# Another order for matmul groups that fill waits: token mixing and modulation units around layer 0's attention

## The reference

```python
# layer 0 mixer, per token tile; h = modulated rms_norm(x)
z = h @ w_in
u, v, q, k, vv = split(z)                 # 512, 512, 512, 128, 128 columns
v = layer_norm(gelu(v), g_vnorm)
mixed = einsum('gts,bnsgc->bntgc', w_s, v_chunks) + b_s
a_out = gelu(u) * mixed
q, k = rms_norm(q, g_q), rms_norm(k, g_k) # latents: then apply_rope on both
b_out = attention with sinks (prompt: dense; latents: window + 128 context keys)
y = concat([a_out, b_out]) @ w_o
# both layers
sh1, sc1, g1, sh2, sc2, g2 = split(silu(cond) @ w_ada + b_ada)
x = x + g1 * y
x = x + g2 * hier_moe(rms_norm(x, g_norm2) * (1 + sc2) + sh2)
```

## Time and profile before

| | |
|---|---|
| three runs | 1081.3, 1087.42, 1085.52 us, median 1085.52 |
| profiled execution | 1081.3 us, of which span 1079.5 |
| mean granted TensorE clock | 0.926 |
| TensorE busy | 913.2 us, 85% |
| VectorE, ScalarE, GpSimd busy | 387.9, 238.7, 120.6 us |
| DMA | 324.97 MB, mean 301 GB/s |

### The profile page before, as it was taken

How to read it: one execution, slowest core, us unless ns; L and a number is a source line. 1 busy time by engine, 2 the same in 40 slices (tenths; PEclk the granted TensorE clock), 3 DMA queues, 4 the chain that set the end, 5 groups by cost and what they waited for, 6 DMA issues and landing times.

```text
span 1079.5 us, 14089 instructions
## 1 busy us (share of the span) xinstructions
PE 913.2 (85%) x5389; PEld 522.4 (48%) x5389; DVE 387.9 (36%) x1096; ACT 238.7 (22%) x598; POOL 120.6 (11%) x131
## 2 busy tenths in 40 slices
PE   5999798977999985998399979997869998859980
PEld 2346346446555553554165544553565555525540
DVE  1112565246522120221334665661456222212214
ACT  3110143120111110111334454341111111101111
POOL 1000001000222211121000000001001222112210
PEclk9999899987999997998699997998869999989996
DMA  9979897385989998998740057008499899999984
GB/s 379 399 294 403 318 417 308 103 276 211 373 313 401 415 416 361 416 413 343 297 149 6 1 193 275 10 7 286 181 404 366 330 410 417 416 392 409 413 338 182
DMA packets 69835, 324.97 MB, mean 301 GB/s; under 512 B 12566, under 2 KB 13590, under 8 KB 46600
## 3 DMA queue, kind: packets, MB, share of 16 engines
q1 hardware_dynamic: 54016, 291.99, 68.0%
q0 software_dynamic: 13328, 25.02, 6.8%
q10 hardware_dynamic: 2432, 7.17, 1.7%
HBM read 318.97 MB, written 26.49 MB: 320 GB/s over the span
## 4 chain that ended last, share of the span: by engine, by line
PE 64%; DMA 21%; DVE 9%; ACT 2%; issue 2%; SPq 1%; POOL 0%; POOLq 0%; DVEq 0%; ACTq 0%
PE psum L760 16%; DMA ring<-in_l_w 13%; PE psum L773 8%; PE psum L956 7%; PE psum L710 4%; DMA ring<-in_l_w_ada 3%; PE psum L1048 3%; PE psum L740 2%; PE psum L1057 2%; PE psum L1008 2%; PE psum L601 2%; PE psum L1089 2%; PE psum L723 1%; DMA scale_shift<-gate_rows_hbm 1%; PE psum L731 1%
## 5 line engine op out<-in xcount | busy, mean ns | idle before, releaser
L760 PE MATMUL psum<-ring,scratch 128*64 128x256 f32 x1920 | 226.8, 390 | 24.6 <-DMA ring<-in_l_w 22.8
L760 PEld LDWEIGHTS psum<-ring,scratch 128*64 128x64 f32 x1920 | 143.6, 140 | 92.9 <-issue 35.2
L1902 DVE TENSOR_TENSOR scratch<-scratch,psum 64x256 f32<-64x256 f32 x64 | 27.2, 424 | 315.0 <-ACT scratch L1304 314.9
L773 PE MATMUL psum<-ring,scratch 128*64 128x512 f32 x496 | 119.9, 604 | 2.6 <-ACT scratch L1308 1.9
L2336 POOL DMA_INDIRECT expert_rows<-scratch,slot_rows x64 | 63.7, 995 | 333.2 <-ACT scratch L1318 321.5
L1304 ACT ACTIVATE scratch<-psum 64x256 f32<-64x256 f32 x64 | 24.0, 375 | 258.4 <-PE psum L760 258.4
L956 PE MATMUL psum<-ring,scratch 128*128 128x512 f32 x192 | 73.1, 539 | 1.3 <-DVE scratch L2023 1.3
L1318 ACT COPY scratch<-psum 128x512 f32<-128x512 f32 x64 | 37.5, 586 | 146.8 <-PE psum L773 146.8
L601 PE MATMUL psum<-ring,scT 128*32 128x512 f32 x320 | 42.9, 662 | 14.7 <-DMA ring<-in_l_w_ada 13.6
L956 PEld LDWEIGHTS psum<-ring,scratch 128*128 128x128 f32 x192 | 36.1, 190 | 36.5 <-issue 35.5
L773 PEld LDWEIGHTS psum<-ring,scratch 128*64 128x64 f32 x496 | 31.0, 136 | 44.9 <-issue 39.9
(11 more groups left out here) (316 smaller groups left out, 1152.0 us busy)
## 6 DMA issues: line engine op xcount, KB each, us to landing
ring<-in_l_w SPq DMA_DIRECT2D x186, 1024.0 KB, 16.6
ring<-in_l_w_ada SPq DMA_DIRECT2D x48, 1024.0 KB, 13.6
ring<-in_l_w_o SPq DMA_DIRECT2D x8, 1024.0 KB, 13.0
ring<-in_l_w_in SPq DMA_DIRECT2D x4, 1024.0 KB, 25.6
gate_rows<-gate_rows_hbm POOLq DMA_DIRECT2D x8, 512.0 KB, 9.8
scale_shift<-gate_rows_hbm POOLq DMA_DIRECT2D x8, 512.0 KB, 11.0
scratch<-expert_rows SPq DMA_DIRECT2D x8, 512.0 KB, 5.0
ring<-in_l_w_in SPq DMA_DIRECT2D x4, 768.0 KB, 13.0
```

What stands on the lines that cost most here:

```text
L760: last = nc.tensor.matmul(ps[64 * n:64 * n + 64, 2 + par, 0:DE], mine[:, k, :], part(w, k * DE, DE), start=k == 0, stop=k == KD - 1)
L773: last = nc.tensor.matmul(ps[64 * n:64 * n + 64, 5 + par, :], hhT[:, par, k, :], part(w2, k * D + n * 512, 512), start=k == 0, stop=k == 1)
```

## The change

TensorE: `mix` leaves the second projection. After it, for each tile, one mix batch is followed by two ada units of layer 0 (16 and 17, 18 and 19, 20 and 21). Then come units 22 and 23, tile 0's transpose, and the transposes of tiles 1 and 2 with no ada units between them. `MORE_ADA` goes; attention has two ada units of layer 1 in each of steps 0 to 7, sixteen in all, units 0 to 3 among them, which stood before tile 2's transpose.

VectorE: `mixed()` for all three tiles moves from ahead of tile 0's q and k to behind it; `modulation(0, 2)` from ahead of tile 2 to behind it; `modulation(1, 0)` from step 1 of attention to step 3. `modulation(1, 1)` stays in step 7. ScalarE's, GpSimd's and SyncE's lists are as before.

```diff
--- before.py
+++ after.py
@@ -336,8 +336,6 @@
         def batches(l):
 
             return [(n, t, i) for n, (t, i) in enumerate(MIX0)]
-
-        MORE_ADA = [range(4 + 2 * n, 6 + 2 * n) if n < 4 else range(8 + n, 9 + n) if n < KD else () for n in range(len(MIX0))]
 
         ATT1 = [("prompt", q, 0) for q in range(4)] + [("sample", i, t) for i in range(KD) for t in (1, 2)]
 
@@ -929,23 +927,9 @@
                 if k % 2:
                     pe.wait_ge(S["mod_act"], k // 2 + 1)
 
-            def mix(t):
-
-                if t == 0:
-                    pe.wait_ge(S["kc_ready"], 1)
-                pe.wait_ge(S["v_ready"], t + 1)
-                if t:
-                    pe.wait_ge(S["a_ready"], t)
-                for g in range(A_GROUPS):
-                    last = nc.tensor.matmul(ps[:, 6, g * P:(g + 1) * P], wsT[:, g, :],
-                                            va[:, t, g * P:(g + 1) * P], start=True, stop=True)
-                last.then_inc(S["mixed_in_psum"], 1)
-
             def project0(first, width, columns, signal):
 
                 for k in range(KD):
-                    if first == U_WIN_QK and k in (3, 5, 7):
-                        mix(k // 2 - 1)
                     unit = first + k // 2
                     arrived(unit)
                     if first == U_WIN_UV:
@@ -970,10 +954,21 @@
             nc.tensor.transpose(ps[:, 6, 0:P], kc[:, :], ident).then_inc(S["kc_in_psum"], 1)
             pe.wait_ge(S["gelu_done"], 1)
             project0(U_WIN_QK, QKV, ((0, 512), (512, QKV)), None)
+            pe.wait_ge(S["kc_ready"], 1)
             for t in range(NT):
-                for l, n in (([(0, 2 * KD + n) for n in range(4)], [(0, 2 * KD + 4 + n) for n in range(4)],
-                              [(1, n) for n in range(4)])[t]):
-                    ada_unit(l, n)
+                pe.wait_ge(S["v_ready"], t + 1)
+                if t:
+                    pe.wait_ge(S["a_ready"], t)
+                for g in range(A_GROUPS):
+                    last = nc.tensor.matmul(ps[:, 6, g * P:(g + 1) * P], wsT[:, g, :],
+                                            va[:, t, g * P:(g + 1) * P], start=True, stop=True)
+                last.then_inc(S["mixed_in_psum"], 1)
+                for n in range(2 * KD + 2 * t, 2 * KD + 2 * t + 2):
+                    ada_unit(0, n)
+            for t in range(NT):
+                if t == 0:
+                    ada_unit(0, 3 * KD - 2)
+                    ada_unit(0, 3 * KD - 1)
                 pe.wait_ge(S["qk_ready"], t + 1)
                 pe.wait_ge(S["z_act_done"], t + 1)
                 for i in range(5):
@@ -983,7 +978,7 @@
 
             pe.wait_ge(S["qkT_ready"], 3)
             pe.wait_ge(S["a_ready"], 3)
-            attention(0, batches(0), lambda n: [ada_unit(1, u) for u in MORE_ADA[n]])
+            attention(0, batches(0), lambda n: [ada_unit(1, 2 * n), ada_unit(1, 2 * n + 1)] if n < KD else None)
             transpose_cat(0)
             transpose_cat(1)
             out_projection(0)
@@ -2037,11 +2032,8 @@
                                      ALU.subtract, ALU.mult))
                 V.tensor_tensor(v, v, gvn[:, :], ALU.mult).then_inc(S["v_ready"], 1)
             modulation(0, 1)
-            mixed()
             for t in range(NT):
 
-                if t == 2:
-                    modulation(0, 2)
                 dve.wait_ge(S["z_act_done"], t + 1)
                 V.tensor_reduce(ss[:, 8:18], sq0.rearrange("p (h d) -> p h d", h=B_HEADS + 2), AX, ALU.add)\
                     .then_inc(S["sums_ready"], 1)
@@ -2066,6 +2058,9 @@
                     link(V.tensor_tensor(qk, qk, gqk[:, :], ALU.mult))
                     rope(heads, rt0.rearrange("p (h d) -> p h d", d=HD), C_R0 + (t - 1) * 2 * HD, HD,
                          B_HEADS + 2).then_inc(S["qk_ready"], 1)
+                if t == 0:
+                    mixed()
+            modulation(0, 2)
             todo = batches(0)
             maxima(0, todo[0])
             for n, b in enumerate(todo):
@@ -2074,8 +2069,8 @@
                 evac_pT(0, b)
                 if n:
                     normalize(0, todo[n - 1])
-                if n in (1, KD - 1):
-                    modulation(1, n // (KD - 1))
+                if n % 4 == 3 and n < KD:
+                    modulation(1, n // 4)
             normalize(0, todo[-1])
             evac_cat(0)
             evac_cat(1)
```

## The result

| | median | runs | profiled execution |
|---|---|---|---|
| before | 1085.52 us | 17, 1078.04 to 1090.24 | 1081.3, span 1079.5, clock 0.926 |
| after | 1090.48 us | 17, 1086.97 to 1098.56 | 1090.64, span 1088.7, clock 0.922 |

The ratio is 1.0068, with a 95% interval of 1.0049 to 1.0087: slower, by 7.4 us (5.3 to 9.4) on 1085.5. It isn't the quotient of the medians, which lie 5.0 us apart; the means of the same 34 times lie 6.5 apart, and those of all 42 executions of the kernel after that are on record (mean 1092.4) and the 17 of the kernel before (mean 1085.0) 7.3. So the size is known to some 2 us. The forecast was 1091.9, +6.4.

The account below looks back on a forecast made before the run. TensorE carried 64% of the chain and was full in attention's middle. Later start +1.2, half clock +2.1, four units +3.4 and modulation -0.3 gave +6.4 us on 1085.5, so 1091.9; own range 1088.5 to 1094.7, stated range 1084 to 1096.

Parts of the forecast that it names:

- Projection shorter, mixes behind it: Second projection on TensorE: without three mix batches it ends 2.7 us sooner; TensorE then waits about 2.7 us for VectorE's gating.
- The store's wait goes, tile 0's transpose is late: Before attention: VectorE's tile 1 waits for TensorE's transpose, not new_l0_k's store, 0.9 us later; scores 1.2 late including slow transpose.
- Clock: TensorE around attention's start: half clock adds 0.6 us in tile 2's transpose and 2.1 in the first steps.
- Four units, one modulation: Attention: a second ada unit in each of steps 4 to 7 costs +3.4 us; layer 1's first modulation in step 3, -0.3.
- rival A: Attention: the four added ada units are hidden in waits, giving +3.0 us, 1088.5; chance 0.15.
- All of it reaches the end: From attention's end on: the output projection has no idle time and DMA waits for its slots, so all +6.4 us remains.
- Rival B: Experts' stage: waits for weights swallow the late attention, giving about 0 us, 1085.5; chance 0.08.
- C: Before attention: VectorE's chain alone sets the start, scores 3.7 us early, attention ends 4.0 early, 1081.5; chance 0.06.
- D: Attention: the clock stays at half for twelve more microseconds, 6 us more, +12.4 in all, 1097.9; chance 0.11.

Follow-up runs that it names:

- e4: Kernel after with tile 0's transpose ahead of ada units 22 and 23 instead of behind them; 1.0073 of the time of the kernel before.
- e8: Kernel after with five, seven and one added matmuls that nobody reads after the transposes of tiles 0, 1 and 2; 1.0042 of the kernel before.
- e3: Kernel after with four added matmuls that nobody reads after tile 0's transpose and six after tile 1's; 1.0082 of the kernel before.
- e9: Kernel after with one ada unit in each of attention's steps 4 to 11 instead of two in 4 to 7, second modulation in step 11; 1.0018 of before.
- e7: Kernel before with tile 0's k stored from a copy, layer 1's units 12 to 15 in steps 8 to 11, second modulation in step 11; 0.9963 of before.

## Why the prediction was right

- *Projection shorter, mixes behind it.* Mix 0 came 30.96 us after the projection's start, where the old order ended it at 33.74: 2.8 sooner, 2.7 forecast. The wait for the first gating was 2.69 us (2.7 forecast).
- *The store's wait goes, tile 0's transpose is late.* Right in kind: VectorE waited for the transpose, 1.88 us. The size was 1.3 us against 0.9. Mix 1 came at 36.55 us where 36.5 was forecast; from there to the transpose TensorE took 7.6 us, not 7.3, and 0.1 of that is a slip in the prediction's adding (122.1 and four units of 0.91 give 125.7, not 125.6). The rest is small change: mixes of 1.06 and 1.09 us for 1.0 each, and VectorE's start 0.86 after the transpose's for 0.8. e4 shows that this transpose was what held the tile. Tile 2 then made up 0.25 without the modulation ahead of it (0.3 forecast), and with the slow last transpose, 0.56 (0.6 forecast), the scores came 1.6 late (forecast 1.2).
- *Clock.* Forecast 0.6 + 2.1. Measured by e8 against the kernel after: 0.56 up to the scores and 1.65 in step 0, 2.2 together. The clock was back 3.6 us after the first scores began (143.2 to 146.8), where 4.3 were assumed; the four other profiles' 2.2 to 2.4 in step 0 lie on the forecast's other side. The Trainium skill's rule that the prediction weighed (TensorE: Matmul & The Clock Gate, "HAM oscillation — how this bites in real kernels") is that a kernel whose bursts are shorter than the waits between them is put back to half rate each time. The second profile of the kernel after agrees in that its clock fell four times between 121 and 197 us. But e3's fall came behind waits of at most 1.3 us with longer bursts between them, and the late ones behind waits of 1.4 and 1.9, which that section's example doesn't cover.
- *Four units, one modulation.* Forecast +3.4 - 0.3. Steps 1 to 3 took 9.54 us instead of 10.65, steps 4 to 7 18.96 instead of 14.85: +3.0 together. These are the starts of the scores that open step 4 and step 8, before and after (timelines of TensorE):

```profile
152.56 0.92 PE L639 MATMUL psum<-scratch 64*128 64x384 f32 x4
...
167.41 0.92 PE L639 MATMUL psum<-scratch 64*128 64x384 f32 x4
```

```profile
157.30 0.92 PE L637 MATMUL psum<-scratch 64*128 64x384 f32 x4
...
176.26 0.92 PE L637 MATMUL psum<-scratch 64*128 64x384 f32 x4
```

The wait for the modulation is 0.62 (0.7 forecast, 1.04 before in the earlier trace rows), which is -0.4. The price of the units lies in their place: with one unit fewer in each of steps 4 to 7 e9 took 3.43 us less there, 0.86 a unit, and with none e7 took only 0.9 less than the kernel before has with one, 0.2 a unit. The prediction's bound of 0 for the second unit, which its range left to rival A, is excluded.
- *All of it reaches the end.* From out to the end of the span it was 895.5 us before and 895.8 after. Rival B is excluded for this pair of profiles. Over all profiles that part takes from 893.7 to 900.7 us at a mean clock of 0.91 or 0.92, so it varies by as much as the whole effect, and why isn't shown. It doesn't absorb: it averages 898.1 over the seven profiles with sixteen units in attention and 896.0 over the six with twelve.

The stretch sums to 1.6 + 1.65 + 3.0 = +6.25 us, forecast 6.4. The ratio's +7.4 (5.3 to 9.4) holds it. That the two sums lie so close is in part luck: tile 0's transpose cost 0.4 more than forecast, and step 0's clock 0.45 less in this profile. What the forecast lacked is that the new 2.7 us wait can itself let the clock fall (+1.6 in two of seven profiles). As an estimate from these profiles that adds some 0.5 us on average, and step 0 as the four other profiles have it adds another 0.5. That these make up the rest of the difference was not shown, and the rest is itself within the interval. Rival A is excluded by the four units' price, C by tile 1's transpose at 49.6 instead of 44.8, and D, half clock for twelve more microseconds, by step 1 at full clock (two units in 1.92 us) in both profiles of the kernel after and in all its variants. Why the clock falls in one execution and not in another of the same kernel stays open.

## What to carry to other kernels

Work that fills waits is free only once for each wait: before moving it, read how much of each step is still wait, and give each step no more than that. Here, in steps 4 to 7, a step's first unit cost 0.2 us and its second 0.86. When a wait disappears from the chain, look in every queue at what the next instruction needs (a transpose behind four units took the store's place). And where TensorE is left with short bursts, price the slower clock in what follows; work that nobody reads, put in the gaps, tells that price. Read that price in the stretch and in more than one profile: here two profiles of one unchanged kernel differed by 2.3 us at the same landmark.

## What the runs showed of the chip

The granted clock fell without one long pause: in e3 TensorE was busy 10.5 of 13 us, its longest waits were 1.3, 1.1 and 0.8 us, and by 144 it was at half. With waits of 0.4 and 0.2 us there (e8) it stayed full. In attention it fell in some profiles behind waits of 1.4 us and in others not. Five transposes of 128x128 in float32 took 0.76 us at full clock and 1.33 at half.
